# Narrow projections formed tokens by columns: tokens as weights, high and low weight parts side by side as moving operand

## What is computed

```
h = rms_norm(x, pre_mix_norm)
proj = h @ w_in                      # [256, 1024] @ [1024, D_IN]
z, xbc, dt_raw, sb_qkv, nsa_q, nsa_kv, nsa_gate, merge_gate = split(proj)
dt   = softplus(dt_raw + dt_bias)    # 16 columns
gate = sigmoid(nsa_gate)             # 24 columns
...
f_logit = (rmsnorm(x, g) @ w_in_2)[..., -8:] + b_f      # 8 columns
cum = cumsum(log_sigmoid(f_logit), axis=1)
```

## Time and profile before

| | |
|---|---|
| median of 3 runs | 853.65 us (852.85 to 855.14) |
| the profiled execution, its time | 852.56 us |
| its span in the profile | 850.8 us |
| mean granted TensorE clock | 0.998 of full speed |
| busy share of the span: TensorE, VectorE, ScalarE, GpSimd | 98%, 70%, 56%, 5% |

### The profile page before, as it was taken

The page is one execution under the profiler, slowest core; times in us unless marked ns, Lnnn a source line. Parts: engine busy times, 40 slices in busy tenths (PEclk is TensorE's granted clock), DMA queues, the critical chain, the costliest instruction groups (busy, mean ns, idle before and its releaser), DMA issues.

```text
span 850.8 us, 13793 instructions
## 1 busy us (share of the span) xinstructions
PE 835.9 (98%) x5334; PEld 737.9 (87%) x5334; DVE 597.2 (70%) x796; ACT 473.0 (56%) x688; POOL 46.6 (5%) x49
## 2 busy tenths in 40 slices
PE   7999999999999999999999999999999999999997
PEld 7999999888777888899999998898888888888885
DVE  5548988748676576798767777878664786666665
ACT  5457873349666344666545556565575554444442
POOL 0025920000000000000000000000000000000000
PEclk9999999999999999999999999999999999999999
DMA  9634453333434456374555555254325355555431
GB/s 355 247 134 142 156 203 119 129 142 139 149 105 161 155 199 240 104 263 153 199 194 172 178 198 208 91 193 150 132 92 193 106 221 198 198 195 191 179 126 49
DMA packets 22163, 143.75 MB, mean 169 GB/s; under 512 B 2928, under 2 KB 3188, under 8 KB 5728
## 3 DMA queue, kind: packets, MB, share of 16 engines
q1 hardware_dynamic: 19440, 136.13, 44.0%
q0 software_dynamic: 1808, 4.73, 1.6%
q10 hardware_dynamic: 864, 2.17, 0.7%
HBM read 141.96 MB, written 1.84 MB: 169 GB/s over the span
## 4 chain that ended last, share of the span: by engine, by line
PE 90%; ACT 4%; DVE 3%; issue 2%; DMA 1%; DVEq 0%; SPq 0%; ACTq 0%
PE pj L469 15%; PE pj L472 9%; PE pj L471 9%; PE pa L949 7%; PE pa L950 7%; PE pa L951 7%; PE pj L473 6%; PE pj L474 6%; PE pj L1167 5%; PE pj L1169 2%; PE pa L531 2%; ACT w_hi L1213 2%; PE po L1167 2%; PE pj L596 2%; PE pj L598 1%
## 5 line engine op out<-in xcount | busy, mean ns | idle before, releaser
L1752 DVE TENSOR_TENSOR w_lo<-w_raw,w_hi 128x2048 fp32r<-128x2048 f32 x127 | 289.1, 2287 | 50.7 <-ACT w_hi L1213 50.2
L1213 ACT ACTIVATE w_hi<-w_raw 128x2048 fp32r<-128x2048 f32 x127 | 242.4, 1910 | 66.7 <-PE pa L951 21.8
L469 PE MATMUL pj<-a_hl,w_hi 128*128 128x256 f32 x656 | 186.8, 285 | 0.9 <-DVE w_lo L1752 0.9
L472 PE MATMUL pj<-a_hl,w_lo 128*128 128x256 f32 x656 | 185.6, 283 | 0.0
L471 PE MATMUL pj<-a_hl,w_hi 128*128 128x256 f32 x656 | 185.6, 283 | 0.0
L469 PEld LDWEIGHTS pj<-a_hl,w_hi 128*128 128x128 f32 x656 | 125.8, 192 | 2.5 <-issue 2.0
L471 PEld LDWEIGHTS pj<-a_hl,w_hi 128*128 128x128 f32 x656 | 125.8, 192 | 0.4
L472 PEld LDWEIGHTS pj<-a_hl,w_lo 128*128 128x128 f32 x656 | 125.8, 192 | 0.0
L949 PE MATMUL pa<-w_hi,a_hl 128*128 128x512 f32 x280 | 109.5, 391 | 0.0
L950 PE MATMUL pa<-w_lo,a_hl 128*128 128x512 f32 x280 | 109.2, 390 | 0.0
L951 PE MATMUL pa<-w_hi,a_hl 128*128 128x512 f32 x280 | 109.0, 389 | 0.0
(11 more groups left out here) (286 smaller groups left out, 1196.7 us busy)
## 6 DMA issues: line engine op xcount, KB each, us to landing
w_raw<-stream SPq DMA_DIRECT2D x126, 1024.0 KB, 4.8
area<-gains POOLq DMA_DIRECT2D x4, 512.0 KB, 3.9
cst<-consts SPq DMA_DIRECT2D x1, 1093.0 KB, 9.6
x_tok<-x_in SPq DMA_DIRECT2D x2, 512.0 KB, 4.8
w_raw<-stream ACTq DMA_DIRECT2D x4, 256.0 KB, 6.4
w_raw<-stream ACTq DMA_DIRECT2D x1, 1024.0 KB, 8.4
area<-cmpw POOLq DMA_DIRECT2D x1, 1024.0 KB, 5.5
out<-x_tok SPq DMA_DIRECT2D x4, 256.0 KB, 2.0
```

Source lines behind the costliest of these rows:

```text
L469: pe.matmul(out_, a[0], a[1], start=first, stop=False)
L472: return pe.matmul(out_, wl, ah, start=False, stop=last)
L1213: act.activation(w_hi[:, slot, :], w_raw[:, slot, :], ACT.Copy).then_inc(S("w_hi_done"), 1)
L1752: dve.tensor_tensor(w_lo[:, slot, :], w_raw[:, slot, :], w_hi[:, slot, :].bitcast(F32), ALU.subtract)\
```

## The change

The roles of the operands are exchanged. The tokens' activations (128 channels by 128 tokens, a half of the 256) become the stationary operand, and the narrow weights move. The high and the low part of the weights lie side by side for each chunk, so that one matmul multiplies the high activations with both parts (80 or 16 columns), and a second one the low activations with the high part (40 or 8 columns). That is 2 halves by 8 chunks by 2 matmuls = 32 matmuls in place of 24. The result has tokens on partitions already: the two transposes and ScalarE's copy out of PSUM go away. `narrow_out` on VectorE becomes three operations: the part with the low weights times `rcol`, the part with the high weights times `rcol`, and their sum, written straight into `small40` or `fl`.

```
@@ TensorE
             def narrow_products(n):
-                for k in range(KC):
-                    mm = three(po[0:n, 0:T], ws_hi[:, k * n:(k + 1) * n], ws_lo[:, k * n:(k + 1) * n],
-                               a_hi[:, k, :], a_lo[:, k, :], k == 0, k == KC - 1)
-                written(mm, "O")
-
-            def narrow_turn(use, n):
-                claim(pe, "O", use)
-                await_read(pe, "O", "dt" if n == 40 else "flog")
-                src = narrow_dt if n == 40 else narrow
+                w = narrow_weights(n)
                 for tb in range(2):
-                    mm = transpose(po[:, tb * 64:tb * 64 + n], src[0:n, tb * P:(tb + 1) * P])
+                    rows, o = slice(tb * P, (tb + 1) * P), tb * T
+                    for k in range(KC):
+                        pe.matmul(po[:, o:o + 2 * n], a_hi[:, k, rows], w[:, k, :, :], start=(k == 0 and tb == 0), stop=False,
+                                  skip_group_check=True)
+                        mm = pe.matmul(po[:, o:o + n], a_lo[:, k, rows], w[:, k, 0, :], start=False, stop=(k == KC - 1),
+                                       skip_group_check=True)
                 written(mm, "O")
...
             narrow_products(40)
             run_unit(("xbc", 0))
-            narrow_turn("dt_tok", 40)
...
             narrow_products(8)
             run_unit(("dq", 1))
-            narrow_turn("flog_tok", 8)
@@ ScalarE
-            act.activation(ws_hi, prm[:, o:o + 320], ACT.Copy).then_inc(S("ws_hi"), 1)
+            act.activation(narrow_weights(40)[:, :, 0, :], prm[:, o:o + 320].rearrange("p (k n) -> p k n", k=KC), ACT.Copy)\
+               .then_inc(S("ws_hi"), 1)
...
             conv_first(0)
-            await_psum(act, "O", "dt_tok")
-            read(act.activation(small40, po[:, 0:128].rearrange("p (b x) -> p b x", b=2)[:, :, 0:40], ACT.Copy), "O")
             sb_logs(0)
...
+            act.wait_ge(S("narrow_ready"), 1)
             act.activation(gate, small40[:, :, 16:40], ACT.Tanh, scale=0.5).then_inc(S("gate_tanh"), 1)
...
             ahead(("dq", 1))
-            await_psum(act, "O", "flog_tok")
-            read(act.activation(fl, po[:, 0:128].rearrange("p (b x) -> p b x", b=2)[:, :, 0:8], ACT.Copy), "O")
             act.wait_ge(S("flx_ready"), 1)
@@ VectorE
-            def narrow_out(use, n):
-                dst = narrow_dt if n == 40 else narrow
+            def narrow_out(use, n, dst):
+                sums = two(po)
+                scale = rcol.unsqueeze(2).to_broadcast([P, 2, n])
                 await_psum(dve, "O", use)
-                read(tt(dst[0:n, :], po[0:n, 0:T], rbc[0:n, :], ALU.mult), "O")
+                V_.did(tt(narrow_part[n], sums[:, :, n:2 * n], scale, ALU.mult))
+                read(tt(dst, sums[:, :, 0:n], scale, ALU.mult), "O")
+                await_read(dve, "O", use)
+                V_.sync()
+                tt(dst, dst, narrow_part[n], ALU.add).then_inc(S("narrow_ready"), 1)
+                dve.wait_ge(S("narrow_ready"), 1 if n == 40 else 2)
...
-            narrow_out("dt", 40)
+            narrow_out("dt", 40, small40)
             conv_out(0)
-            await_read(dve, "O", "dt_tok")
```

More of the change, by code:

```diff
@@ L157, in program @@
         tiny = sb("tiny", [P, 1024])
-        ws_hi = a_hl[:, 22, :, :].rearrange("p a b -> p (a b)")[:, 0:320]
-        ws_lo = a_hl[:, 23, :, :].rearrange("p a b -> p (a b)")[:, 0:320]
+        ws_flat = a_hl[:, 22:24, :, :].rearrange("p c a b -> p (c a b)")
         rbc = sb("rbc", [P, T])
@@ L242, in program @@
         lf8 = V(54, 2, 16, 8)
-        t5_sb, narrow, narrow_dt = V(20, 384), V(12, T), V(51, T)
+        t5_sb, narrow_part = V(20, 384), {40: V(51, 2, 40), 8: V(12, 2, 8)}
         conv_tap, conv_tap0 = V(57, T), V(56, T)
@@ L290, in program @@
             + [f"n{r}" for r in range(8)] + [f"d{r}" for r in range(4)] + [f"f{r}" for r in range(4)]
-        O_USE = ["rbc0", "dt", "dt_tok", "sb0", "sb1", "y0", "y1", "y2", "y3", "hid", "kc", "t5"] \
+        O_USE = ["rbc0", "dt", "sb0", "sb1", "y0", "y1", "y2", "y3", "hid", "kc", "t5"] \
             + [f"n{j}" for j in range(4)] + ["rbc1", "rbc2",
-               "flog", "flog_tok", "d0", "fcum", "d1", "f0", "f1", "f2", "f3", "rbc3"]
+               "flog", "d0", "fcum", "d1", "f0", "f1", "f2", "f3", "rbc3"]
         USE = {"S": S_USE, "T": T_USE, "O": O_USE}
@@ L330, in mix_turned, with narrow_weights @@
             return mix_banks[h][c // 2][:, (c % 2) * T:(c % 2 + 1) * T]
+        def narrow_weights(n):
+            return ws_flat[:, 0:2 * KC * n].rearrange("p (k v n) -> p k v n", k=KC, v=2)
         def decays(g, part):
@@ L1622, in _ @@
             o2 = PCOLS["ws2"][0]
-            act.activation(ws_hi[:, 0:64], prm[:, o2:o2 + 64], ACT.Copy).then_inc(S("ws_hi"), 1)
+            act.activation(narrow_weights(8)[:, :, 0, :], prm[:, o2:o2 + 64].rearrange("p (k n) -> p k n", k=KC), ACT.Copy)\
+               .then_inc(S("ws_hi"), 1)
             x_root(2)
@@ L1962, in _ @@
             o = PCOLS["ws1"][0]
-            tt(ws_lo, prm[:, o:o + 320], ws_hi.bitcast(F32), ALU.subtract).then_inc(S("ws_ready"), 1)
+            w40 = narrow_weights(40)
+            tt(w40[:, :, 1, :], prm[:, o:o + 320].rearrange("p (k n) -> p k n", k=KC), w40[:, :, 0, :].bitcast(F32),
+               ALU.subtract).then_inc(S("ws_ready"), 1)
             def gate_decay(g):
@@ L2331, in _ @@
             o2 = PCOLS["ws2"][0]
-            tt(ws_lo[:, 0:64], prm[:, o2:o2 + 64], ws_hi[:, 0:64].bitcast(F32), ALU.subtract)\
-                .then_inc(S("ws_ready"), 1)
+            w8 = narrow_weights(8)
+            tt(w8[:, :, 1, :], prm[:, o2:o2 + 64].rearrange("p (k n) -> p k n", k=KC), w8[:, :, 0, :].bitcast(F32),
+               ALU.subtract).then_inc(S("ws_ready"), 1)
             lv = prm_("lam").rearrange("p (a b d) -> p a b d", a=2, b=2)
@@ L2400, in _ @@
             d_soft(0)
-            narrow_out("flog", 8)
+            narrow_out("flog", 8, fl)
             d_probs(0)
@@ L2404, in _ @@
             channel_major(("dq", 1), dq[:, 2:4, :], 64.0 ** -0.5)
-            await_read(dve, "O", "flog_tok")
             tt(fl, fl, prm_("b_f").unsqueeze(1).to_broadcast([P, 2, 8]), ALU.add).then_inc(S("flx_ready"), 1)
```

## The result

The changed kernel takes 860.3 us (median of 4 runs, 859.7 to 861.25); the kernel before takes 853.25 us beside it (4 runs). The ratio is 1.0069 with a 95% interval of 1.0052 to 1.0087: slower by 0.7%. The forecast was 855.0 us with a range up to 857.0 us, so it was wrong: 1.34 us were forecast, about 7 came. In none of the four runs is the mean granted clock above 0.993, where before has 0.998 in its profiled run; the profiled run is the fastest of the four, the other three have 0.990, and where they lost more no trace shows.

A forecast was written before the change was run, and what follows sets the result against it. The prediction took TensorE's own list, busy 98% of the span, as the bound, with a VectorE and ScalarE chain behind the second place. +0.56 and +0.78 us gave +1.34 us on the median of 853.65: 855.0 us, range 852.4 to 857.0.

The forecast's parts named there:

- The step that failed: Both places: 32 new matmuls at 0.112 us, 3.58 us, less the removed work, taken as the whole TensorE cost.
- gain nothing by it: First place: moving 1,920 columns in place of 6,144 saves nothing, since loading 128 stationary columns takes the same slot.
- Bound by TensorE's own list: Whole kernel: TensorE, busy 98% of the span, is the first suspect; work added from 40 to 300 us reaches the end.
- The price of 0.112 us: Each new narrow matmul in both places costs 0.112 us, so 32 of them cost 3.58 us per place.
- quicker loads: Rival, 17%: new matmuls in both places cost 0.076 us each, as with L833; -0.6 us in all, 853.0 us.
- double records: Rival, 10%: each narrow float32r product costs two records like float32, 0.22 us; +8.5 us over both places, 862.2 us.
- First place, +0.56 us: Narrow matmuls from 45.34 us, ahead of unit xbc 0: +3.58 - 2.78 - 0.24 us, going through in full.
- Second place, +0.78 us: Narrow matmuls from 558.01 us, ahead of dq 1: 3.58 - 2.80 us, passing through VectorE and ScalarE to `d_turn(1)`.
- The likeliest case's own range: Whole kernel: forecast of 855.0 us with the spread of earlier runs, given as 854.0 to 856.3 us; chance 65%.
- VectorE and ScalarE, nothing: Both places: three `narrow_out` operations in place of one, and removing ScalarE's copy, change nothing at the end.
- The lower edge: Whole kernel: faster by over 0.3%, under 851.1 us, needs more than any price gives, 3%; range starts at 852.4 us.

The follow-up runs named there:

- e1: The changed kernel with each new matmul's moving operand repeated to 240 or 256 columns in both places; 856.3 us, ratio 1.0026 to the kernel before.
- e4: Only the first place changed against the kernel before, its narrow matmuls in pairs among the matmuls of unit xbc 0; 853.72 us, ratio 1.0004.
- e12: The kernel before plus 64 extra matmuls of 8 moving columns ahead of the first sliding-window apply (81 us); 867.81 us, ratio 1.0163.
- e2: Only the first place changed, the second as in the kernel before; 856.5 us, ratio 1.0027.
- e3: Only the second place (forget gates) changed, the first as in the kernel before; 859.2 us, ratio 1.0044.
- e9: The kernel before with the moving operand of the `kct` scores repeated to 80 columns in place of 16; 853.76 us, ratio 0.9995.
- e5: Against the kernel before: high and low narrow weights side by side as stationary operand, 16 matmuls for 24 per place, transposes kept; 854.82 us, ratio 1.0009.
- e11: e1 with the `kct` scores widened to 80 moving columns in place of 16; 855.62 us, ratio 1.0021 to the kernel before.
- e10: e5 with the `kct` scores widened to 80 moving columns in place of 16; 853.56 us, ratio 1.0000 to the kernel before.
- e7: The kernel before plus 32 extra matmuls of 8 moving columns ahead of the first sliding-window apply (81 us); 859.82 us, ratio 1.0065.
- e8: The kernel before plus 32 extra matmuls of 256 moving columns ahead of the first sliding-window apply (81 us); 858.86 us, ratio 1.0057.

## Why the prediction was wrong, point by point

**The step that failed** is the one from the price of the slots to the sum: 32 matmuls by 0.112 us in each place, less what is removed, was taken as all that the row does to TensorE. That holds only with the clock at 2.4 GHz on the instructions behind, which the prediction assumed without saying so, nor did any of its rivals. It noted that the columns moved fall from 6,144 to 1,920 in the first place and took this to be neutral ("gain nothing by it"). In fact it costs: the fall of the clock behind each row is worth 1.5 us, more than either net term. e1 (columns put back, 4.3 us less than after in the profiled runs), e4 (same matmuls, mixed) and e12 (longer row) show that it is the row of narrow matmuls that does it, and all 21 runs of after, e2 and e3 lost clock, none above 0.996. The remaining parts of the 6.9 us: 1.58 us for the stretch near 194 us, which e3 shows without any narrow matmul of the change ahead of it and which e9 suggests is part of the spread of before, and 0.88 us at the start, whose cause is open. That after, e2, e3 and e5 all have the stretch near 190 us in their profiled runs, while the clocks of before's runs leave room for it in 28 of 79, is more than chance readily gives; what makes it likelier there stays open.

**Bound by TensorE's own list:** right. Everything added to it, the clock's loss too, came out at the end: 6.9 us more span for 7.8 us more busy time.

**The price of 0.112 us:** right, 3.49 us for 32 and one record each. The weight loads last as long as the large units' (the groups of its loads by form; the units' stand at 194 ns in the same view):

```profile
L655 PEld LDWEIGHTS po<-a_hl 128*128 128x128 f32 x32 | 6.2, 195 | 0.0
L653 PEld LDWEIGHTS po<-a_hl 128*128 128x128 f32 x32 | 6.1, 192 | 0.4 <-issue 0.3
```

So the quicker loads (17%) and the double records (10%) both didn't come. The quicker loads had been read from L833's 0.076 us. Neither its 16 moving columns nor quicker loads explain that: with 8 and 16 columns the new matmuls stand 0.11 us apart, and L833's loads last 187 ns in the mean, L786's 192. What differs is its 64 rows of weights; no run varies them alone.

**First place, +0.56 us:** 0.48 us without the stretch at half clock (1.95 with it). **Second place, +0.78 us:** about 0.9 us without it (2.40 with it), and by the way forecast: the scaling of dq 1 moved from 566.76 to 573.56 us and `d_turn(1)` from 576.83 to 583.64, both 6.8 us, waiting for VectorE as before, now 1.21 us. The two together are about the forecast +1.34 us. The medians of e11 and e9 bear the sum out: both have the widened scores and keep the clock in every run, and they differ by 855.62 - 853.76 = 1.9 us. By the prediction's sum with e1's rows it would be 3.59 + 4.01 - 5.58 - 0.24 = 1.8 us, an estimate.

**The likeliest case's own range** was added up loosely: 0.8 below and 1.5 above 855.0 us give 854.2 to 856.5, not 854.0 to 856.3. That changes nothing here.

**VectorE and ScalarE, nothing:** right. `narrow_out` takes three operations of 0.17 us, over at 566.76, before the reciprocal at 567.18 that ScalarE's exponentials release.

**The lower edge.** That the change could be faster had 3%; no form tried is. e4, with the first place alone and mixed, equals before (0.9988 to 1.0019), and so does e10.

## What to carry to other kernels

A change on a full TensorE is priced in two parts: the slots, and what the new order does to the granted clock of the instructions behind. Where many weight loads with few moving columns come to stand in a row, read the clock by stretch right behind; here each such row cost 1.5 us in instructions that nobody had touched, more than the edit's own 0.5 to 0.9 us. Mixing the narrow matmuls among wide ones kept the clock in the profiled runs at no cost of its own (0.116 us each), and so did widening their moving operand: to 240 columns it cost nothing (0.112 us each), to 256 a little (0.125). Neither made the change faster than the kernel before. When a kernel's own runs fall into groups with different granted clocks, look for such a row in it before you compare tenths of a per cent.

## What the runs showed of the chip

- TensorE's clock falls to 1.2 GHz without any idle time: 64 matmuls with weights of 128 by 128 and 8 moving columns, 2.00 of 2.00 us busy, brought it from 1.00 to 0.50 within the row (the median record took 354 ns, where those of 8 columns in after took 259 in the mean; first to last start 11.0 us for 63 distances). The Trainium skill ("TensorE: Matmul & The Clock Gate", HAM oscillation — how this bites in real kernels) tells of the clock lost in waits for data between groups of matmuls; e10's fall in TensorE's wait of 2.06 us is near to that, though it waits there for VectorE, and e5 has such a wait of 2.1 us without a fall. The falls in after and e12 come with no wait at all, and there the measurement decides.
- Whether the clock falls behind a row of 32 differs: at 565 us it fell with one of 16 and 8 moving columns, at 82 us it didn't with one of 8 in the profiled run. What decides it isn't settled here, nor where the other runs of e7, and those of e8, lost clock.
- A matmul with 128 by 128 weights costs about the same 0.11 us with 8, 16, 40, 80 and 240 moving columns (rows of 32 in after and e1), and 0.125 us with 256 in e1's second place.
- The start: the first eight transposes of `x_tok` took 1.09 us in the profiled runs of before, e4, e5 and e9, and 1.97 us in those of the ten others, whose first unit starts at 10.69 to 10.94 us in place of 9.80 to 10.18. Among the ten are e7, e8 and e12, whose TensorE has the same list as in before up to 80 us, so it doesn't need the change. The Trainium skill (same page, Part 1: The HAM clock gate (the "warmup" mystery)) says that the count of matmuls at the lower level at a kernel's start differs from run to run. The durations fit that, but the granted clock of these traces reads 1.00 there, so they don't show it. A profiled difference under 1 us between two kernels is therefore to be read from a landmark behind the start.
